# Two-layer decoder with routed experts: 32 expert blocks of up to 104 rows become 24 blocks of 128 rows in four 32-column groups

## What is computed

```python
g_sel = argmax(x2 @ w_rg + b_rg)                    # one group of 4
e_logit = (x2 @ w_re + b_re)[8 experts of that group]
top_p, top_i = top_k(softmax(e_logit), 2)           # two of its experts
gates = g_w * top_p / sum(top_p)
...
hid = silu(xb @ w_eg[e]) * (xb @ w_eu[e])           # 1024 -> 256, 32 experts
out = hid @ w_ed[e]                                 # 256 -> 1024
y = sum over the two slots of gate * out
```

## Time and profile before

| | |
|---|---|
| median of 3 runs (lowest, highest) | 2886.36 us (2873.0, 2890.05) |
| span of the profiled execution | 2865.1 us |
| its own time beside the span | the profile gives none; the median is 21.3 us above the span |
| busy PE / weight loads / DVE / ACT / POOL | 91% / 63% / 41% / 25% / 14% |
| mean granted TensorE clock | 0.952 |
| experts of layer 0, first `gate_up` to last `down` | 1022.85 to 1387.78 us |
| experts of layer 1 | 2424.66 to 2790.10 us |
| bytes read / written in HBM | 355.55 MB / 44.55 MB |

### The profile page before, as it was taken

How to read it: one execution, slowest core, us unless ns; L and a number is a source line. 1 busy time by engine, 2 the same in 40 slices (tenths; PEclk the granted TensorE clock), 3 DMA queues, 4 the chain that set the end, 5 groups by cost and what they waited for, 6 DMA issues and landing times.

```text
span 2865.1 us, 38998 instructions
## 1 busy us (share of the span) xinstructions
PE 2605.3 (91%) x15964; PEld 1817.8 (63%) x15964; DVE 1176.1 (41%) x2208; ACT 720.4 (25%) x1448; POOL 413.7 (14%) x561
## 2 busy tenths in 40 slices
PE   7999988899999889999699999888899997999994
PEld 5645556556667578887465455565666765888872
DVE  4155557543223433233351555584323334333225
ACT  1124453331003301111311244443211222111113
POOL 0004225110000011111100123251000000111111
PEclk9999998898999989999799999989999997999996
DMA  4001001342141268898410100113223214888954
GB/s 162 17 17 32 5 5 34 115 184 74 37 163 68 105 233 324 321 339 329 180 54 4 38 11 8 34 39 151 111 89 127 82 45 175 294 330 329 331 205 184
DMA packets 76932, 385.65 MB, mean 135 GB/s; under 512 B 25086, under 2 KB 31868, under 8 KB 65724
## 3 DMA queue, kind: packets, MB, share of 16 engines
q1 hardware_dynamic: 53164, 304.90, 29.2%
q0 software_dynamic: 23040, 76.59, 7.6%
q10 hardware_dynamic: 576, 2.10, 0.2%
HBM read 355.55 MB, written 44.55 MB: 140 GB/s over the span
## 4 chain that ended last, share of the span: by engine, by line
PE 73%; DVE 10%; PEld 4%; ACT 4%; issue 4%; DMA 2%; POOLq 1%; POOL 1%; PEldq 1%; SPq 0%; DVEq 0%; ACTq 0%
PE ps L1319 16%; PE ps L667 12%; PE ps L1332 8%; PE ps L1237 4%; PE ps L725 4%; PE ps L805 4%; PEld ps L667 4%; PE ps L817 2%; PE ps L833 2%; PE ps L1003 2%; PE ps L1308 2%; PE ps L783 2%; DVE arena L1993 1%; DVE nmax L1894 1%; PE ps L936 1%
## 5 line engine op out<-in xcount | busy, mean ns | idle before, releaser
L667 PE MATMUL ps<-arena,ring 128*128 128x352 f32 x1704 | 508.4, 461 | 3.4 <-DVE arena L1783 2.4
L1319 PEld LDWEIGHTS ps<-arena 128*128 128x128 f32 x4096 | 470.8, 193 | 35.7 <-issue 35.7
L1319 PE MATMUL ps<-arena 128*128 128x104 f32 x4096 | 470.5, 276 | 4.9 <-issue 2.5
L667 PEld LDWEIGHTS ps<-arena,ring 128*128 128x128 f32 x1704 | 324.8, 191 | 184.9 <-issue 5.7
L1332 PE MATMUL ps<-arena 128*104 128x512 f32 x512 | 230.4, 593 | 2.6 <-ACT arena L1713 2.6
L1713 ACT ACTIVATE arena<-ps 104x1024 f32<-104x1024 f32 x64 | 65.5, 1023 | 470.7 <-PE ps L1332 470.7
L2419 DVE TENSOR_SCALAR arena<-arena 128x208 f32<-128x208 f32 x64 | 17.2, 269 | 401.2 <-ACT arena L1706 401.2
L2554 POOL DMA_INDIRECT arena<-xrow,arena x64 | 70.5, 1102 | 671.7 <-PE ps L1308 353.9
L1332 PEld LDWEIGHTS ps<-arena 128*104 128x104 f32 x512 | 81.9, 170 | 104.0 <-issue 104.0
L805 PE MATMUL ps<-arena 96*128 96x512 f32 (+3 forms) x384 | 147.1, 493 | 0.0
L1481 ACT ACTIVATE ring<-ps 128x512 f32<-128x512 f32 (+2 forms) x192 | 87.3, 490 | 127.2 <-PE ps L817 127.1
(11 more groups left out here) (411 smaller groups left out, 3587.5 us busy)
## 6 DMA issues: line engine op xcount, KB each, us to landing
arena<-in_w_e SPq DMA_DIRECT2D x64, 3072.0 KB, 13.5
ring<-in_ring SPq DMA_DIRECT2D x56, 512.0 KB, 3.6
arena<-yrow SPq DMA_DIRECT2D x16, 1024.0 KB, 7.7
arena<-in_mem_k SPq DMA_DIRECT2D x16, 512.0 KB, 7.1
arena<-in_mem_v SPq DMA_DIRECT2D x16, 512.0 KB, 10.4
xrow<-arena SPq DMA_DIRECT2D x16, 512.0 KB, 6.3
x<-in_x SPq DMA_DIRECT2D x3, 1408.0 KB, 11.5
out_y<-arena SPq DMA_DIRECT2D x3, 1408.0 KB, 5.6
```

The lines of the kernel that those rows point to most:

```text
L667: mm = pe.matmul(ps[:, (j % 2) * NCH + c, 0:CH], ring[:, j // per, (j % per) * units + k, :], src[:, k, tok], start=k == k0, stop=k == uni ...
L1319: mm = pe.matmul((gate_ps if m < 2 else up_ps)[:, m % 2, 0:rows], w_e[j][:, at:at + P], xb_t[:, p, k, 0:rows], start=k == 0, stop=k == KT - 1)
```

## The change

The experts' slots are packed: expert `e` owns the 96 slots from `96 * e` on (`CAP` is 96), and the 3072 slots are cut into `NB` = 24 blocks of 128 rows. A block is four groups of 32 rows, and since 96 is three times 32, each group belongs to one expert; a block touches two experts (`experts_of`).

- `gate_up` turns around: the 32 rows of a group are stationary (128x32), 512 columns of that group's expert are moving, and the result lands on 32 partitions of the PSUM bank. The four groups stand next to each other in the program; 8 steps of the sum by 4 groups = 32 matmuls of 512 columns. `down` is cut into the same four groups: 16 matmuls in place of 4.
- The hidden rows now come out with rows on partitions, so there is a new step, `turn_h` (2 transposes on PE) with its eviction `keep_h` on ACT, between `hidden` and `down`. PE's order is `gate_up(n)`, `turn_h(n - 1)`, `turn_x(n + 1)`, `down(n - 1)`.
- `gate_up` waits for the weights of both experts of its block. Expert `e`'s buffer is free once `last_block(e)` has been through `down`; SP waits for that before it requests expert `e + 4`.
- SP requests experts 1 and 2 right behind the nine row stores, and no longer waits for the first gathers.
- The loops over blocks and over overflow blocks are written out, with a branch for each of the (now up to 24) overflow blocks.

The diff, cut to its core:

```diff
-CAP = 104
-OVER = 20
-NBLK = NE + OVER
+CAP = 96
+GRP = 32
+NB = NE * CAP // P
+OVER = 24
+NBLK = NB + OVER
...
-        h_e, h_t = view(VG + 6 * D, 2, P), view(VG + 6 * D + 2 * P, 2, 2, P)
+        h_e, h_t = view(VG + 6 * D, 2, 2 * P), view(VG + 6 * D + 4 * P, 2, P)
...
-        up_done, dn_done, dn_evac = sem("up_done"), sem("dn_done"), sem("dn_evac")
+        ht_done, ht_evac, dn_done, dn_evac = sem("ht_done"), sem("ht_evac"), sem("dn_done"), sem("dn_evac")
...
-        gate_ps, up_ps = (ps[:, b, 0:2 * P].rearrange("p (m t) -> p m t", m=2) for b in (2, 3))
+        def experts_of(n):
+
+            return [(n * P + GRP * g) // CAP for g in range(P // GRP)]
+
+        def last_block(e):
+
+            return (CAP * (e + 1) - 1) // P
+
...
-                for p in range(2):
-                    sp.wait_ge(xb_full[p], 16)
                 load_w(1, 1)
                 load_w(2, 2)
-                with sp.Fori(0, NE // 4 - 1) as i:
-                    for j in range(4):
-
-                        n = 4 * i + j
-                        sp.wait_ge(dn_done, n + 1)
-                        sp.sem_inc(turn, 1)
-                        load_w(j, n + 4)
+                for e in range(4, NE):
+                    sp.wait_ge(dn_done, last_block(e - 4) + 1)
+                    load_w(e % 4, e)
 
                 n_over = sp.value_load(over_i[0:1, 0:1], min_val=0, max_val=OVER)
                 with sp.If(n_over > 0):
-                    with sp.Fori(0, OVER // 4) as i:
-                        for j in range(4):
-                            o = 4 * i + j
-                            with sp.If(n_over > o):
-                                sp.wait_ge(dn_done, NE + o)
-                                sp.sem_inc(turn, 1)
-                                e = sp.value_load(over_i[0:1, bass.ds(o + 1, 1)], min_val=0, max_val=NE - 1)
-                                load_w(j, e)
+                    for o in range(OVER):
+                        with sp.If(n_over > o):
+                            sp.wait_ge(dn_done, last_block(NE - 4 + o) + 1 if o < 4 else NB + o - 3)
+                            e = sp.value_load(over_i[0:1, o + 1:o + 2], min_val=0, max_val=NE - 1)
+                            load_w(o % 4, e)
...
-                def turn_x(n, p, full, rows=CAP):
-
-                    pe.wait_ge(xb_full[p], full)
-                    pe.wait_ge(tx_evac, n)
+                def turn_x(n):
+
+                    pe.wait_ge(xb_full[n % 2], 16 * (n // 2 + 1))
+                    if n >= 1:
+                        pe.wait_ge(tx_evac, n)
                     for k in range(KT):
-                        mm = pe.transpose(xt_ps[:, k, 0:rows], xb[0:rows, p, k * P:(k + 1) * P], ident[0:rows, 0:rows])
+                        mm = pe.transpose(xt_ps[:, k, :], xb[:, n % 2, k * P:(k + 1) * P], ident)
                     mm.then_inc(tx_done, 1)
 
-                def gate_up(n, p, j, full, rows=CAP):
-
-                    pe.wait_ge(we_full[j], full)
+                def gate_up(n, experts, loads):
+
+                    for e in sorted(set(experts)):
+                        pe.wait_ge(we_full[e % 4], 16 * loads(e))
                     pe.wait_ge(tx_evac, n + 1)
-                    pe.wait_ge(h_ready, n)
-                    for m in range(4):
-                        for k in range(KT):
-                            at = k * 512 + m * P
-                            mm = pe.matmul((gate_ps if m < 2 else up_ps)[:, m % 2, 0:rows], w_e[j][:, at:at + P], xb_t[:, p, k, 0:rows],
-                                           start=k == 0, stop=k == KT - 1)
-                        if m == 1:
-                            mm.then_inc(gu_done, 1)
-                    mm.then_inc(up_done, 1)
-
-                def down(n, p, j, rows=CAP):
+                    if n >= 2:
+                        pe.wait_ge(h_ready, n - 1)
+                    for k in range(KT):
+                        for g, e in enumerate(experts):
+                            r = slice(GRP * g, GRP * (g + 1))
+                            mm = pe.matmul(ps[r, 2 + n % 2, :], xb_t[:, n % 2, k, r], w_e[e % 4][:, k * 512:(k + 1) * 512],
+                                           start=k == 0, stop=k == KT - 1, skip_group_check=True)
+                    mm.then_inc(gu_done, 1)
+
+                def turn_h(n):
 
                     pe.wait_ge(h_ready, n + 1)
+                    if n >= 1:
+                        pe.wait_ge(ht_evac, n)
+                    for m in range(2):
+                        mm = pe.transpose(ps[:, 6, m * P:(m + 1) * P], h_e[:, n % 2, m * P:(m + 1) * P], ident)
+                    mm.then_inc(ht_done, 1)
+
+                def down(n, experts):
+
+                    pe.wait_ge(ht_evac, n + 1)
                     pe.wait_ge(dn_evac, n + 1)
                     for f in range(2):
                         for k in range(2):
                             at = KT * 512 + k * D + f * 512
-                            mm = pe.matmul(ps[0:rows, 4 + f, :], h_t[:, p, k, 0:rows], w_e[j][:, at:at + 512], start=k == 0, stop=k == 1)
+                            for g, e in enumerate(experts):
+                                r = slice(GRP * g, GRP * (g + 1))
+                                mm = pe.matmul(ps[r, 4 + f, :], h_t[:, k, r], w_e[e % 4][:, at:at + 512],
+                                               start=k == 0, stop=k == 1, skip_group_check=True)
                     mm.then_inc(dn_done, 1)
 
-                def block(n, j, i, j1, i1, more=True):
-
-                    gate_up(n, j % 2, j, 16 * (i + 1))
-                    if more:
-                        turn_x(n + 1, j1 % 2, 16 * (2 * i1 + j1 // 2 + 1))
-                    down(n - 1, (j + 1) % 2, (j + 3) % 4)
-
-                turn_x(0, 0, 16)
-                gate_up(0, 0, 0, 16)
-                turn_x(1, 1, 16)
-                with pe.Fori(0, NE // 4 - 1) as i:
-                    for j in range(1, 5):
-                        nxt = j + 1
-                        block(4 * i + j, j % 4, i + j // 4, nxt % 4, i + nxt // 4)
-                for n in range(NE - 3, NE):
-                    block(n, n % 4, n // 4, (n + 1) % 4, (n + 1) // 4, more=n < NE - 1)
-                down(NE - 1, 1, 3)
+                def loads_of(e):
+
+                    return e // 4 + 1
+
+                turn_x(0)
+                for n in range(NB):
+                    gate_up(n, experts_of(n), loads_of)
+                    if n >= 1:
+                        turn_h(n - 1)
+                    if n + 1 < NB:
+                        turn_x(n + 1)
+                    if n >= 1:
+                        down(n - 1, experts_of(n - 1))
+                turn_h(NB - 1)
+                down(NB - 1, experts_of(NB - 1))
                 n_over = pe.value_load(over_i[0:1, 0:1], min_val=0, max_val=OVER)
                 with pe.If(n_over > 0):
-                    with pe.Fori(0, OVER // 4) as i:
-                        for j in range(4):
-                            with pe.If(n_over > 4 * i + j):
-                                n = NE + 4 * i + j
-                                turn_x(n, j % 2, 16 * (NE // 2 + 2 * i + j // 2 + 1), P)
-                                gate_up(n, j % 2, j, 16 * (NE // 4 + i + 1), P)
-                                down(n, j % 2, j, P)
+                    for o in range(OVER):
+                        with pe.If(n_over > o):
+                            n, experts = NB + o, [o % 4] * (P // GRP)
+                            turn_x(n)
+                            gate_up(n, experts, lambda e: NE // 4 + o // 4 + 1)
+                            turn_h(n)
+                            down(n, experts)
...
-                def gate_exp(n, rows=CAP):
+                def gate_exp(n):
                     act.wait_ge(gu_done, n + 1)
-                    act.activation(h_e[:, :, 0:rows], gate_ps[:, :, 0:rows], ACT.Exp, scale=-1.0).then_inc(ge_ready, 1)
-
-                def keep_y(n, p, rows=CAP):
+                    act.activation(h_e[:, n % 2, :], ps[:, 2 + n % 2, 0:2 * P], ACT.Exp, scale=-1.0).then_inc(ge_ready, 1)
+
+                def keep_h(n):
+
+                    act.wait_ge(ht_done, n + 1)
+                    act.activation(h_t.rearrange("p m t -> p (m t)"), ps[:, 6, 0:2 * P], ACT.Copy).then_inc(ht_evac, 1)
+
+                def keep_y(n):
 
                     act.wait_ge(dn_done, n + 1)
                     act.wait_ge(y_out, n + 1)
-                    act.sem_inc(turn, 1)
-                    act.activation(y_sb[0:rows, p, :].rearrange("p (a n) -> p a n", a=2), ps[0:rows, 4:6, :], ACT.Copy).then_inc(dn_evac, 1)
+                    act.activation(y_sb[:, n % 2, :].rearrange("p (a n) -> p a n", a=2), ps[:, 4:6, :], ACT.Copy).then_inc(dn_evac, 1)
...
                     gate_exp(n)
-                    keep_y(n - 1, (n - 1) % 2)
-                keep_y(NE - 1, 1)
-                act.wait_ge(y_out, NE)
+                    if n >= 1:
+                        keep_h(n - 1)
```

(80 more changed lines are left out.)

36 lines of the change are left out of this document (15 added, 21 removed).

## The result

The changed kernel took 3179.64 us (median of 4 runs, 3164.73 to 3184.44) against 2887.11: 1.1044 times as long, 95% interval 1.1013 to 1.1076. I had forecast 3221 us and a range of 3150 to 3300. The profiled execution's own time is 3164.73 us, 1.8 above its span.

A forecast was written before the change was run, and what follows sets the result against it. PE was taken to bound the kernel before. Stages 275, early requests 6, overflow block 34 and branches 20 made +335 on a 2865.1 us span: 3200, plus 21.3 around it, 3221 us; range 3150 to 3300.

The forecast's parts named there:

- The step that decided: Weight requests in the expert stage: issued right before the gate_up that needs them, giving 14 bare loads a layer.
- A block of PE: PE's work on one block of the expert stage: 11.7 to 12.5 us, taken as 12.0.
- A bare load: PE's wait before gate_up for a weight load with nothing to hide it: 12.9 us, bounds 11.6 and 14.
- The clock: PE's slow restart after each bare load, its clock having fallen: 2.1 us each, upper bound 3.1.
- The stage: One layer's expert stage: 502.6 us against 364.9, so +137.7 a layer and +275 us for two.
- The early requests: Experts 1 and 2 requested earlier, their loads beside the first gathers: 3 us a layer, +6 in all.
- The overflow block: After layer 0's regular blocks: one overflow block with 4 rows, +34 us, bounds 25 and 45.
- The branches: PE's jumps over 23 written-out overflow blocks in layer 0: about 1 us each, +20 us after hiding.
- that rival: Each of PE's 23 overflow jumps costs 3.58 us, 82 us instead of 20: 3283 us; chance 0.11.
- Weights ahead of need: Rival for the expert stage: requests go out a block sooner, DMA sets the pace: 2862 us; chance 0.04.
- the point from which it decides: For weights ahead in the expert stage: with a stop shorter than 5.1 us, the stage is faster than before.

The follow-up runs named there:

- e3: The changed kernel with a fifth weight buffer, each request one block before its need: 2896.10 us, 1.0063 times the kernel before.
- e1: The changed kernel loading only the weights of experts 0 to 3 in each layer, all blocks kept: 2878.84 us, 1.0001 times the kernel before.
- e2: The changed kernel with 12 matmuls of constants on PE before each gate_up that waits for weights: 3128.57 us, 1.0874 times the kernel before.
- e11: The kernel before with experts 1 and 2 requested right behind the row stores: 2879.30 us, 1.0015 times the kernel before.
- e8: The changed kernel with experts 1 and 2 requested only after the first two gathers landed, as before: 3193.23 us, 1.1095 times the kernel before.
- e4: The changed kernel with the overflow blocks' branches nested, so one jump leaves all later ones: 3132.24 us, 1.0876 times the kernel before.
- e6: The changed kernel with five weight buffers, nested branches and each expert's weights requested in two parts: 2780.60 us, 0.9665 times the kernel before.
- e10: e6 with down parts requested ahead of gate and up parts that become free one matmul group earlier: 2761.64 us, 0.9600 times the kernel before.
- e9: The changed kernel (four buffers) with nested branches and two-part requests, down parts ahead of later-needed gate and up parts: 2980.98 us, 1.0360 times the kernel before.

## Why the prediction was right, point by point

**The step that decided was the request.** Two bare loads in three blocks, at the blocks named and at none else, is what the trace shows, and e3 is its test: one more buffer takes 284 us off. e1 puts the loss of the stage at 188 us in layer 0 against the 210 of the forecast.

**A block of PE** was set at 12.0 us and is 11.68: 64 records in 6.87 us are 0.107 each, four times as fast as one record of 0.43, and the lower value that I had for `gate_up` was the right one. At 0.107 us a record of a group and 0.109 a transpose (0.87 for 8) the four parts would add up to 11.4 us, so all changes of mode in a block cost some 0.3 us at most. By the rule that I had weighed (the Trainium skill, TensorEngine Tiling (Array Packing), Key Properties) a drain comes at each change; a drain of the 1.2 us a block that I had priced is excluded by the trace, one inside the 0.3 us is not. This term was 8 us a layer too large.

**A bare load** was set at 12.9 us, and over layer 0's 14 waits it averages 11.2 (10.6 to 12.7). In layer 1 it averages 11.5. The step that was mis-sized is the landing of 12.4: between a lone load's 11.1 and the crowded 13.4 I leaned on the second, but at the wait the queue is all but empty, and the 14 loads that PE waits for in layer 0 land in 10.3 to 12.4 us, 11.0 in the mean. The waits are 23 and 19 us shorter than forecast in the two layers, the largest single error of the sum.

**The clock** was set at 2.1 us for each restart; the 14 `gate_up` behind waits average 9.11 us, 2.24 more than 6.87, and e2 gives back 50 to 55 us for 28 of them, 1.8 to 2.0 each.

**The stage** was 502.6 us in the forecast, 473.7 measured.

**The early requests** were set at +6. e11 shows no change that can be told. The changed kernel's first `gate_up` came 5.8 us earlier than before in layer 0, but that is no gain of theirs: the trace was 8.1 us ahead already before the routing. From the first gather's issue to the first `gate_up` it is 11.8 and 10.7 us in the two layers, where the kernel before has 10.3 in both, so they cost at most 2 us in all, and by e8 the old place would have cost 5 us a layer more.

**The overflow block** was there in layer 0 and its chain, set at +34, measured +29.5 in e4.

**The branches** were set at 20 us and cost 49.5. The row that I leaned away from, PE's single jump of 3.4 to 3.7 us, was the one that told the truth: 19 of 23 jumps take about 3.1 us. I had given that rival 0.11. It is no wait for matmuls still queued on PE, since the last `down` was through at some 1520 us and the jumps go on to 1578. I read it as a fetch: each of the 19 long jumps has one packet of 16 KB in the instruction queue, and the 4 short ones have none. The two jumps of the earlier trace rows have one such packet each as well, which the prediction had left open. That they coincide is shown; that one waits for the other is inferred. The rule of the Trainium skill that I had set beside this rival (Runtime: NRT & Kernel Launch, Instruction fetch mechanics), that a taken branch out of the fetched window waits for a DMA fetch, agrees with it, the price being 3.1 us here. POOL's branches over its own short blocks stayed at 34 to 53 ns.

The errors had opposite signs: the stages came out 55.5 us under the forecast, the overflow block and its jumps 25 over it, and the early requests with the untouched stretches 7 under it, together 37 of the 41 us. The other 4 lie around the span: the median is 16.7 us above it, not 21.3. Part of the nearness is luck.

**The rivals.** Weights ahead of need did not happen in this kernel, but e3, e6 and e10 are that case, built: the point from which it decides, a stop of 5.1 us, fits e9: its waits average 5.9 us, the slow clock behind them comes on top, and its stage in layer 1 is 403 us, still longer than the 365 before. DMA, whose bound I had put at 369 GB/s, never became the bound: e10 moves 368 GB/s at a share of 0.91, and PE is busy for 284 of its stage's 291 us.

## What to carry to other kernels

When tiles are packed so that one spans two weights, count again for each buffer which step frees it and which step first needs its next content: a four-deep rotation that was three blocks ahead became none. A change that takes work from the bound engine pays only as far as its inputs are requested ahead. Put requests in a queue in the order of need, and let rare blocks be left by one jump, not passed one by one.

## What I had not expected of the hardware

Four matmuls of 32 columns by 512 in 32-bit floats ran four abreast (0.107 us a record against 0.43), with transposes of the full array on either side at a cost of at most 0.3 us a block. A branch on PE that passes over some 58 matmuls cost 3.1 us in 19 of 23 cases and 0.2 to 0.4 us in the others, and in e4 one that passed over 23 such blocks cost 3.8. And 12 matmuls of constants in front of each wait made the kernel 51 us faster.
